# Sums of squares of the head norms as two fp32r products of a high and a low half

## The reference

```python
h  = rmsnorm(x, mix_norm[l])
sq, sk, sv, gq, gk, gv, gg, glr, mq = jnp.split(h @ w_in[l], splits, axis=-1)
# swa: q (8 heads of 64), k (2 heads of 64); memory attention: q and k (4 heads of 64)
q = rmsnorm(q, q_gain)   # over the 64 entries of each head
k = rmsnorm(k, k_gain)
def rmsnorm(x, g):
    x32 = x.astype(jnp.float32)
    y = x32 * lax.rsqrt(jnp.mean(x32 * x32, axis=-1, keepdims=True) + EPS)
    return (y * g.astype(jnp.float32)).astype(x.dtype)
```

## Time and profile before

| | us |
|---|---|
| median of 3 runs | 1718.77 |
| lowest and highest | 1718.09, 1720.46 |
| the profiled execution | 1718.25 |
| its span, first to last instruction | 1716.5 |

### The profile page before, as it was taken

How to read it: one execution, slowest core, us unless ns; L and a number is a source line. 1 busy time by engine, 2 the same in 40 slices (tenths; PEclk the granted TensorE clock), 3 DMA queues, 4 the chain that set the end, 5 groups by cost and what they waited for, 6 DMA issues and landing times.

```text
span 1716.5 us, 24866 instructions
## 1 busy us (share of the span) xinstructions
PE 1698.9 (99%) x8329; PEld 1385.5 (81%) x8329; DVE 1124.1 (65%) x1575; ACT 718.2 (42%) x1350; POOL 531.5 (31%) x432
## 2 busy tenths in 40 slices
PE   9999999999999999999989999999999999999999
PEld 6788888888888889887766688888888888888887
DVE  7975555555498596347888863985555555569654
ACT  5533333333344563232177832543333333334442
POOL 0454445544130141000056612145554444310000
PEclk9999999999999999999999999999999999999999
DMA  7342222233774431120100122222233322485434
GB/s 207 72 151 92 98 98 92 104 117 121 271 245 125 157 98 68 50 85 25 37 2 2 38 99 99 74 99 92 92 110 121 111 104 92 171 282 160 136 103 166
DMA packets 101694, 191.71 MB, mean 112 GB/s; under 512 B 11491, under 2 KB 13972, under 8 KB 101612
## 3 DMA queue, kind: packets, MB, share of 16 engines
q1 hardware_dynamic: 100528, 188.48, 32.4%
q0 software_dynamic: 848, 2.10, 0.9%
q10 hardware_dynamic: 236, 0.06, 0.0%
HBM read 139.74 MB, written 50.86 MB: 111 GB/s over the span
## 4 chain that ended last, share of the span: by engine, by line
PE 92%; DVE 3%; ACT 1%; POOL 1%; issue 1%; DVEq 0%; ACTq 0%
PE ps L56 29%; PE ps L57 29%; PE ps L58 29%; PE ps L1675 1%; PE ps L1603 1%; PE ps L1307 1%; ACT glu L1808 1%; POOL Pg L1975 1%; DVE loT L373 1%; PE ps L1593 1%; PE ps L1724 0%; DVE ring L502 0%; PE ps L1712 0%; PE ps L1398 0%; PE ps L1698 0%
## 5 line engine op out<-in xcount | busy, mean ns | idle before, releaser
L502 DVE TENSOR_TENSOR ring<-w_raw,ring 128x512 fp32r<-128x512 f32 x240 | 239.9, 1015 | 219.0 <-ACT ring L497 218.9
L56 PE MATMUL ps<-hiT,ring 128*128 128x512 f32 x672 | 261.5, 389 | 1.5 <-DVE ring L502 1.5
L58 PE MATMUL ps<-hiT,ring 128*128 128x512 f32 x672 | 261.5, 389 | 0.0
L57 PE MATMUL ps<-loT,ring 128*128 128x512 f32 x640 | 249.0, 389 | 0.0
L56 PE MATMUL ps<-down_ring 128*128 128x512 f32 x616 | 239.7, 389 | 0.0
L57 PE MATMUL ps<-down_ring 128*128 128x512 f32 x616 | 239.6, 389 | 0.0
L58 PE MATMUL ps<-down_ring 128*128 128x512 f32 x616 | 239.6, 389 | 0.0
L56 PE MATMUL ps<-hiB,ring 128*128 128x512 f32 x576 | 224.9, 390 | 0.0
L58 PE MATMUL ps<-hiB,ring 128*128 128x512 f32 x576 | 224.1, 389 | 0.0
L497 ACT ACTIVATE ring<-w_raw 128x512 fp32r<-128x512 f32 x240 | 150.4, 628 | 165.4 <-PE ps L58 164.0
L876 ACT ACTIVATE down_ring<-down_raw 128x512 fp32r<-128x512 f32 x176 | 109.1, 630 | 226.0 <-DMA down_raw<-act_dram 184.2
(11 more groups left out here) (259 smaller groups left out, 3004.1 us busy)
## 6 DMA issues: line engine op xcount, KB each, us to landing
down_raw<-act_dram SPq DMA_DIRECT2D x154, 256.0 KB, 2.6
w_raw<-in_w_gate SPq DMA_DIRECT2D x88, 256.0 KB, 3.0
w_raw<-in_w_up SPq DMA_DIRECT2D x88, 256.0 KB, 3.1
act_dram<-actT SPq DMA_DIRECT2D x88, 256.0 KB, 2.0
act_dram<-act SPq DMA_DIRECT2D x66, 256.0 KB, 2.0
wd<-in_w_down SPq DMA_DIRECT2D x44, 256.0 KB, 4.9
wd_mirrored<-in_w_down SPq DMA_DIRECT2D x33, 256.0 KB, 4.6
p_raw<-in_w_proj SPq DMA_DIRECT2D x15, 512.0 KB, 3.6
```

The lines of the kernel that those rows point to most:

```text
L56: nc.tensor.matmul(out, w_hi, x_hi, start=first, stop=False, skip_group_check=resumed)
L57: nc.tensor.matmul(out, w_hi, x_lo, start=False, stop=False, skip_group_check=resumed)
L58: return nc.tensor.matmul(out, w_lo, x_hi, start=False, stop=last, skip_group_check=resumed)
L502: nc.vector.tensor_tensor(ring[:, e % RING, 1, :], op_source(e), ring[:, e % RING, 0, :].bitcast(F32), ALU.subtract).then_inc(op_ready, 1)
```

## The change

Each of the 16 squares is computed twice on ScalarE, once into `square_hi` (rounded to fp32r) and once in float32 into `glu` as before. GpSimd subtracts the high half from it, in place, which gives `square_lo` in fp32r. The sum is two fp32r products into the same bank. `head_ones` is converted once to fp32r, by ScalarE. The waits on `head_squared` count both squares and that conversion. The semaphore of GpSimd's one product in the projection is renamed and counts the low halves as well. The four sums at the end of the mixing stage keep one fp32 product.

```diff
+        head_ones_raw = phase(("head_ones_raw", [P, P], F32))[0]
+        head_ones = sb("head_ones", [P, P], F32R)
...
+        square_hi = place(180 * KB, ("square_hi", [P, 2, HALF], F32R))[0]
+        square_lo = place(196 * KB, ("square_lo", [P, 2, HALF], F32R))[0]
...
         def head_square(act, i, src, w):
             wait(act, head_summed, i - 1)
+            if i < GLA_OUT:
+                nc.scalar.activation(square_hi[:, i % 2, 0:w], src, ACT.Square).then_inc(head_squared, 1)
             nc.scalar.activation(head_buffer(i, w), src, ACT.Square).then_inc(head_squared, 1)
 
+        def squared_count(i):
+            return 2 + i + min(i + 1, GLA_OUT)
+
+        def head_square_lo(pool, i, w):
+            pool.wait_ge(head_squared, squared_count(i))
+            nc.gpsimd.tensor_tensor(square_lo[:, i % 2, 0:w], head_buffer(i, w), square_hi[:, i % 2, 0:w].bitcast(F32),
+                                    ALU.subtract).then_inc(pool_product, 1)
+
         def head_sum(pe, i, w):
-            pe.wait_ge(head_squared, i + 1)
-            if i < GLA_OUT:
-                wait(pe, head_normed, i - 1)
-            nc.tensor.matmul(head_bank(i, w), head_ones[:, :], head_buffer(i, w), start=True,
-                             stop=True).then_inc(head_summed, 1)
+            if i >= GLA_OUT:
+                pe.wait_ge(head_squared, squared_count(i))
+                nc.tensor.matmul(head_bank(i, w), head_ones[:, :].bitcast(F32), head_buffer(i, w), start=True,
+                                 stop=True).then_inc(head_summed, 1)
+                return
+            wait(pe, head_normed, i - 1)
+            pe.wait_ge(head_squared, squared_count(i))
+            nc.tensor.matmul(head_bank(i, w), head_ones[:, :], square_hi[:, i % 2, 0:w], start=True, stop=False)
+            pe.wait_ge(pool_product, i + 2)
+            nc.tensor.matmul(head_bank(i, w), head_ones[:, :], square_lo[:, i % 2, 0:w], start=False, stop=True
+                             ).then_inc(head_summed, 1)
...
             nc.scalar.activation(memT[:], memT[:], ACT.Square).then_inc(mem_split, 3)
+            nc.scalar.activation(head_ones[:], head_ones_raw[:], ACT.Copy).then_inc(head_squared, 1)
...
-            nc.gpsimd.tensor_tensor(ggT[:, 0, :], gqk[:, 0, :], gqk[:, 1, :], ALU.mult).then_inc(diag_product, 1)
+            nc.gpsimd.tensor_tensor(ggT[:, 0, :], gqk[:, 0, :], gqk[:, 1, :], ALU.mult).then_inc(pool_product, 1)
+            for i in range(GLA_OUT):
+                head_square_lo(pool, i, width(i))
             mix_pool(pool)
```

More of the change, by code:

```diff
@@ L76, in build @@
         ones = sb("ones", [P, P])
-        head_ones = sb("head_ones", [P, P])
+        head_ones_raw = phase(("head_ones_raw", [P, P], F32))[0]
+        head_ones = sb("head_ones", [P, P], F32R)
         eps = sb("eps", [P, 1])
@@ L182, in build @@
         (tok_summed, proj_ready, proj_taken, mem_hi_ready, mem_lo_ready, mem_split, mem_summed, mem_rooted, mem_normed, gate_ready,
-         gate_biased, gate_min, gate_log, gate_summed, diag_product, diag_summed, diag_taken, head_squared, head_summed,
+         gate_biased, gate_min, gate_log, gate_summed, pool_product, diag_summed, diag_taken, head_squared, head_summed,
          head_rooted, head_normed, out_gate_tanh, out_gate_ready, out_added, gla_gated, gla_hi_ready, gla_lo_ready, state_cleared,
@@ L186, in build @@
             "tok_summed proj_ready proj_taken mem_hi_ready mem_lo_ready mem_split mem_summed mem_rooted mem_normed gate_ready "
-            "gate_biased gate_min gate_log gate_summed diag_product diag_summed diag_taken head_squared head_summed "
+            "gate_biased gate_min gate_log gate_summed pool_product diag_summed diag_taken head_squared head_summed "
             "head_rooted head_normed out_gate_tanh out_gate_ready out_added gla_gated gla_hi_ready gla_lo_ready state_cleared "
@@ L203, in build @@
                   (gate_bias[:], gate_bias_in.rearrange("n a -> a n").to_broadcast([P, P])), (gate_up_w[:], gate_up_in),
-                  (ident[:], ident_in), (head_ones[:], head_ones_in)]
+                  (ident[:], ident_in), (head_ones_raw[:], head_ones_in)]
         NCONST = len(consts)
@@ L1416, in proj_tensor @@
                     pe.wait_ge(gains_scaled, 4)
-                    pe.wait_ge(diag_product, 1)
+                    pe.wait_ge(pool_product, 1)
                     for t in range(NB):
```

## The result

| | before | changed |
|---|---|---|
| median, us (13 runs each) | 1718.77 | 1723.53 |
| lowest and highest | 1717.98, 1720.91 | 1719.53, 1726.77 |
| span of the profiled execution | 1716.5 | 1722.2 |

The ratio is 1.0023, 95% interval 1.0015 to 1.0030: slower, by 2.6 to 5.2 us. A second measurement of the same two kernels on another chip (last experiment) gave 1.0013, 1.0004 to 1.0022. The forecast was 1722.1, in the range 1717.5 to 1727.5.

What follows compares the result with a forecast made beforehand. TensorE bounds the kernel, 99% busy, but the closed VectorE-ScalarE loop, lengthened 5.9 us less a 0.8 us earlier start, overtakes it; scores come 3.35 us later: 1718.25 + 3.35 = 1721.6, 1722.1 as a median, range 1717.5 to 1727.5.

Steps and rivals of the forecast that it cites:

- What bounds the kernel: Projection: TensorE fills the chain of waits, but VectorE and ScalarE form a closed loop, 13.12 us per two groups against 12.68.
- ScalarE's Square: Each of the 16 head groups: one more Square ahead of Sqrt, lengthening every loop with a square by 0.535 us.
- TensorE's saving: Sums of squares: two fp32r products take 0.45 us instead of 0.86, saving 6.1 us if TensorE never waits.
- head start: Two short sums and one long are over before the closed loop begins, so it starts 0.8 us earlier.
- The loop's end: Eleven loops grow 5.9 us, less 0.8: last looped evict at 852.5, last norm ends 861.8, scores at 862.0, +3.35 us.
- GpSimd's part at nothing: Low-half subtraction, 1.2 to 1.45 us per group, ready by 3.4 us after the evict started; costs nothing.
- B: Rival: GpSimd's new work slows VectorE or ScalarE, another 0.27 us in each of eleven loops, 3.0 us: 1725.1; chance 0.1.
- C: Rival: low half collides with p_lo, four of them losing up to 1.45 us each: +5.8, 1727.9; chance 0.05.
- D: Rival: two fp32r products take as long as the fp32 one; only the 0.8 us is lost: 1722.9; chance 0.04.
- TensorE's waits: TensorE waits before each sum after q3's second half, 7.6 us, and 1.9 us before the first block's scores.
- Rival A: TensorE stays the bound, the second Square hides in the loop, full 6.1 us gain: 1712.6; chance 0.08, part gain 0.08.
- 3.4 us bound: Two parts in a thousand of the whole time, what a measurement can tell from no change; forecast median 1722.1 against 1722.2.

Runs made afterwards that it cites:

- Sqrt first: Changed kernel with ScalarE's Sqrt of the group two before ahead of this group's Squares: 1716.78 us, ratio 0.9978; same swap in the kernel before: 1720.42 us, ratio 1.0001.

## Why the prediction was right

*What bounds the kernel.* Right, and the point of it all: the chain of waits was pure TensorE, and VectorE's and ScalarE's loop, only 3 us behind it, set the time as soon as it grew.

*ScalarE's Square.* Forecast 0.535 us a loop, measured 6.51 - 5.99 = 0.52 and 7.66 - 7.13 = 0.53. The queue's spacing was the price, not the record of 0.63.

*TensorE's saving.* Forecast 0.45 for two products, measured 0.48, so the 6.1 us were mis-sized: with the loop open 5.5 came out. Of the head start of 0.8 us the evict of 776.86 shows 0.88 on the span's clock (775.98), 0.75 counted from the reciprocal of rstd_tok.

*The loop's end.* Forecast 852.5, measured 852.20; the last norm forecast to end at 861.8, measured 860.85 + 0.75 = 861.60; the scores forecast at 862.0, measured 861.74. Eleven loops grew by 5.71 us in all instead of 5.9. The sum came out as +3.28 instead of +3.35, counted from the reciprocal of rstd_tok; part of this closeness is luck. TensorE started 0.14 us behind the last norm instead of 0.2, the head start was smaller than forecast, and the forecast counted from 858.66, the start in the chain, where the time line has 858.59; these partly cancel.

*GpSimd's part at nothing.* Right: 1.29 us each (forecast 1.2 to 1.45), ready 3.2 us after the evict started, and doubling it changed nothing. Rivals B and C are out: the reciprocal is 3.37 us in both kernels, and the p_lo of this stretch 1.22. D is out too, with 0.48 for the pair. The reciprocal agrees with the Trainium skill, "SBUF — State Buffer", section "Who interferes with whom": an instruction of VectorE with at most one input in SBUF, outside the two-port perf modes, doesn't contend with GpSimd. The case of C, a VectorE instruction with two inputs in SBUF beside GpSimd's reads, never came about here for p_lo: none of the ten overlaps a subtraction of GpSimd in time.

*TensorE's waits.* Right in kind, in releaser and in the first sum that waits, the one behind q3's second half. They show as 5.8 us before sums and 1.5 before the scores, forecast 7.6 and 1.9. Part of the difference is how they are counted: they start at the modelled end of a record, which lies 0.16 us behind the interval of a running TensorE (0.39 against 0.23), so an estimate is 6.9 and 1.7. Rival A, the full gain, needed the loop to be open; Sqrt first opened it and gave 5.5 of the 6.1 us.

*What the forecast left out.* The clock. The median is 1.4 us over the forecast of 1722.1. I took the granted clock for a constant because the kernel before shows it at full speed on the page. But a 9 there stands for 90% or more, and the ten-microsecond stretches of the same trace show 0.86 from 690 to 700 us. The changed kernel's own executions lie between 1719.53 us (mean clock 1.000) and 1726.77 (0.996), so the clock belonged in the sum as a term of 0 to 3 us, estimated from these. By their ratios the first measurement of the pair is +4.0 us and the second +2.2, on either side of the forecast's +3.35; at equal mean clock the second gives 2.9 to 3.5. On which side of the 3.4 us bound a single measurement falls is luck.

## What to carry to other kernels

A chain of waits that shows one engine only doesn't say how close the next loop is. Before you shorten the bound engine's work, follow each other engine once around its loop, in its program order, and compare its period with the bound's; here it was 13.12 against 12.68 us for two groups, held apart by a lead of 3 us. Work added to such a loop costs its full queue spacing, however idle the engine looks (ScalarE was busy 42% of the span), and reordering two instructions of it may be worth more than the change itself: here 8.8 us in the interval (+3.28 to -5.54).

Where kernels differ by a few us, compare a stretch between two instructions, or executions of equal mean clock, and not the medians alone.

## What the runs showed of the hardware

TensorE's clock falls from the higher level to the lower one (from 1.00 to 0.50 in stretches of one us) in two places of this kernel, with and without the change, in some executions and not in others. The first is near 700 us, at the sums over mem, which begin with one-column matmuls: 9 of the 14 profiles have it, for 3 to 7 us, and TensorE's records leave no gap there (10.00 of 10.00 us busy at a granted clock of 0.91, changed kernel). The second is in the first mixing block, behind a wait of 1.5 us for qg among matmuls of 64 to 256 columns. 5 of the 10 profiles without products in that wait have it, the changed kernel in one of its two, and the kernel before with Sqrt first among them (0.86 from 870 to 880 us). The wait of 1.5 us is in the others too: the kernel before has 1.53 and no fall. From the evict of the last group to the end the five take 852.7 to 853.6 us and the other nine 850.2 to 851.5, so the fall costs about 2 us. TensorE's time line at the sums over mem, kernel with Sqrt first:

```profile
696.82 1.84 PE L1414 MATMUL ps<-ones,memT 128*128 128x1 f32 x8
698.53 6.16 PE L1417 MATMUL ps<-memT,ones 128*128 128x256 f32 x16
```

The four profiles with products of 512 columns in the block's wait have no fall there. With such products in the waits of the projection instead it was still there, in one profile.

The Trainium skill, "TensorE: Matmul & The Clock Gate", section "Part 1: The HAM clock gate", ties the clock to how busy the engine has been recently. The runs bear this out only in part. The fall in the block is absent where the wait is filled, but also in half of the profiles where it isn't, and near 700 us it comes while the records leave no gap. A record's end is modelled, so what sets the clock there stays open.
